# A two-block network in one kernel: the first four projections taken from x instead of from its norm, and other places in the queues for shift sums, a turn and activations of the mixer

## The chip, the cores and the metric

One core of a Trainium2 chip runs the whole program in one launch. The metric is the device time of one execution in microseconds, the median of several. A core has TensorE (matrix products), VectorE, ScalarE and GpSimd, each with its own queue of instructions that it works off in order, SyncE, which issues most DMAs, and 16 DMA engines. Engines wait for one another through semaphores, and a waiting instruction holds up everything queued behind it on its engine.

## What is computed

All in float32, 512 tokens by 1024 channels. The first layer is differential attention with 16 heads; then come an adaptively modulated ffn, a token mixer (pools, convolutions, gated delta rule in 8 heads) and a second ffn. Cut to what matters here:

```python
h = rms_norm(x, g)                          # x * rsqrt(mean(x*x)+eps) * g
q, k, v, z = split(h @ w_in)                # 4 x 2048 columns
q = rms_norm(q per 64, q_g) / 8; k = rms_norm(k per 64, k_g)
o = differential_attention(q, k, v, alibi)
x = x + (rms_norm(o, head_g) * 0.8 * silu(z)) @ w_out
shift, scale, gate = split(silu(c) @ ada_w + ada_b)        # for 3 sublayers
h = rms_norm(x, g0) * (1 + scale0) + shift0
x = x + 0.5 * gate0 * (silu(h @ w_gate) * (h @ w_up)) @ w_out1
h = rms_norm(x, g1) * (1 + scale1) + shift1
x = x + gate1 * token_mixer(h)              # h @ w -> pools, conv q/k/v, b/a, z, gates
h = rms_norm(x, g2) * (1 + scale2) + shift2
x = x + 0.5 * gate2 * ffn2(h)
out = rms_norm(x, final_g)
```

## The kernel before

Channels lie on the 128 partitions, tokens along the free axis, so x is eight chunks X[0..7] of 128x512. A **tile** is 128 output columns: for each step k (128 rows of the weight) TensorE makes three products (lines 1111, 1112, 1114): high part of the weight by high part of the operand, high by low, low by high, all rounded to a faster format. So every operand is split: ScalarE rounds (hi_of), VectorE takes the difference (lo_of). The weights of eight steps, 512 KB, are a **slot**. SyncE fetches slots in order into four buffers; the step `split` rounds one, three slots ahead of its use. A step of eight k is thus followed by its output (`out_...`) and a split.

The order is written by class Plan: a list of steps, and each engine walks the same list and takes from it what is its own. In the mixer and in attention, small steps are put between the k of the tiles by number: `at(tick, step)`, where a tick is one k, or SCHED. A step's place in the list is its place in the queue of **every** engine that has a part in it.

**Start** (lines 1024 to 1064, 1411, 1828 to 1866). SyncE fetches small data, constants, the eight chunks of x, then the slots. ScalarE squares the chunks, TensorE sums them into ps[7], ScalarE makes the root (logarithm and exponential), VectorE scales each chunk by gain and root, ScalarE rounds, VectorE subtracts: eight chunks in turn, with three splits behind the third. Then `two` runs q0 and k0 alternating, and v0 follows. `rstd` norms a head's q and k (a sum on TensorE, line 1162, from the parts that `sq_lo` finishes), `scores`, `weigh`, `turnw` and `pv` are the attention proper, `ada` computes the modulation from weights that GpSimd fetches.

**Later norms** (`raw_start`). The last residual chunk is late, so the first two or three tiles behind a norm run on x times gain ("raw", rhs "r"); their results are multiplied by the root, and the shift's part is added as a vector: `shift_row` (VectorE, line 1464, straight from the fetched weights) and `shift_sum` (TensorE sums the rows, line 1128; VectorE copies the result, line 1470). `norm_rs` makes the root, `norm_c` a run of chunks of h (VectorE 1479 and 1483, ScalarE 1899), needed from the first tile with rhs "h" on. Before, `shift_sum` stood in the last residual tile.

**Mixer.** Two raw pool tiles, a narrow tile ba (16 columns), pool 2, `baturn` (TensorE turns ba; ScalarE and VectorE make beta and g from it, a chain of small operations), pool 3, with `pool_mid` products in between (line 1224; GpSimd fetches their weights), `decays`. Then conv tiles for k, q and v: `out_conv` evicts, `conv_taps` (VectorE 1696 to 1701) follows 2 ticks behind the tile's last k, `conv_act` (ScalarE 2039, with `conv_sq` 2046) 7 ticks, `v_turn` 13. Sessions of four heads follow: `l2_sum` (TensorE 1252), `l2`, `prep_x`, `prep_k`, `prep_q`; a triangular solve on VectorE whose data go out and back through memory; inverse and recurrence.

Of the kernel before, what the change touches and what calls it, by code (L numbers as in the profile page):

```python
# [19 lines left out]
NRAW = 4  # L20
# [110 lines left out]
class Plan:  # L131
# [52 lines left out]
    def two(self, t0, t1, then=None, ahead=False):  # L184
        self.slot(t0, 0)
        self.slot(t1, 0)
        for k in range(8):
            self.add("mm", t=t0, k=k)
            self.add("mm", t=t1, k=k)
        for t in (t0, t1):  # L190
            t.done = t.slots[-1] + 1
            if ahead:
                self.add("split", j=t.slots[0] + NSPL)
        for t in (t0, t1):
            self.add("out_" + t.kind, t=t, done=t.done, **t.more)
            if not ahead:
                self.add("split", j=t.slots[0] + NSPL)
            if t is t0 and then is not None:
                then()

# [12 lines left out]
    def raw_start(self, n, t0, t1, t2=None):  # L213
# [4 lines left out]
        for k in range(8):  # L218
# [3 lines left out]
            self.add("mm", t=t0, k=k)  # L222
# [39 lines left out]
    def norm(self, n, kind):  # L262
        self.add("norm", n=n, kind=kind, stat=8 + 2 * n, rs=self.sig("rs"), nv=8 * n, nl=8 * n)
        if kind != "out":
            for name in ("nv", "nh", "nl"):
                self.count[name] = self.count.get(name, 0) + 8

    def attention(self):
# [3 lines left out]
        for c in range(8):  # L272
            self.square(0, c)
        self.norm(0, "plain")
        add("rnd", both=[sig("rnd"), sig("rnd")])
        st = [{} for _ in range(HEADS)]
        qk_free, rs_free = [("nl", 8)] * 4, [("nl", 8)] * 4
# [4 lines left out]
        def tile(kind, col, **d):  # L282
            return Tile(kind, src("l0_w_in", col), pb.take()[1], "h", None, n=0, **d)
# [13 lines left out]
        def v(h):  # L297
            d = dict(h=h, ve=sig("ve"))
            st[h]["v"] = d
            t = tile("v", 4096 + 128 * h, d=d)  # L300
# [76 lines left out]

        small = {}
        for i in range(HEADS + 3):
# [10 lines left out]
            if i < HEADS:  # L390
                put(SCHED["lo"][1], sq_lo, i, "k")
# [14 lines left out]
            for n in range(NADA):  # L406
                if (SCHED["ada"] + 21 * n) // 24 == i:
                    put((SCHED["ada"] + 21 * n) % 24, ada, n)
# [26 lines left out]
    def out0(self):  # L435
# [18 lines left out]
        def square(c):  # L454
# [7 lines left out]
              (7, 8): lambda: self.shift_row(1, 2, first + 2), (7, 13): lambda: self.shift_sum(1, 3)}  # L462
# [14 lines left out]
    def ffn(self, sub, w_in, w_out):  # L477
# [31 lines left out]
        for c in range(8):  # L509
            r = sig("xr")  # L510
            t = Tile("res", src(w_out, 128 * c, 22), pb.take()[1], "a", ("xr", r), c=c, xr=r, sub=sub, f=f, back=None)
            for k in self.steps_of(t):
# [6 lines left out]
                if n == 1 and c == 7 and k == 16:  # L519
                    self.shift_sum(2, 2)  # L520
# [4 lines left out]
    def mixer(self):  # L525
# [17 lines left out]

        self.raw_start(n, pool(0, "r"), pool(1, "r"))
        add("feed_pool")
        t = Tile("ba", src("mix_w_in_2", 4608, cols=16), wk.take()[1], "h", ("bd", 1), n=n)
        self.whole(t)
        for k in self.steps_of(pool(2)):
            if k == 5:
                pool_mid(0)  # L550
        add("baturn", bank=wk.take()[1])
        self.move("saved")
        for k in self.steps_of(pool(3)):
            if k == 5:
                pool_mid(1)
# [51 lines left out]
        def conv(which, h):  # L607
# [85 lines left out]
        at(7, pool_mid, 2)  # L693
        at(11, lambda: add("decays", bank=wk.take()[1]))
# [1577 lines left out]
```

## Time and profile before

| | |
|---|---|
| three runs | 1914.41, 1915.87, 1916.69 us; median 1915.87 |
| the profiled execution | 1915.09 us |
| its span, first to last instruction | 1913.3 us |
| TensorE products | 1873.1 us busy (98%), 8923 |
| VectorE | 988.9 us (52%) |
| ScalarE | 815.8 us (43%) |
| GpSimd | 124.2 us (6%) |
| mean granted TensorE clock | 0.994 |

A page of the profile gives the busy time of each engine, the span in 40 slices, the DMA queues, the chain that ended last and the costliest groups of instructions. Line numbers are the kernel's; L1820 and L1404 are the helpers of all roundings and differences. Since TensorE is busy nearly throughout, the views that matter are those of its idle time: a list of what each engine waited for, and timelines in order of time.

### The profile page before, as it was taken

How to read it: one execution, taken by the hardware profiler on the slowest of the kernel's cores; microseconds unless marked ns; L12 is line 12 of the kernel's file. 1: busy time of each engine (PE TensorE's matmuls, PEld its weight loads, DVE VectorE, ACT ScalarE, POOL GpSimd, SP SyncE). 2: the span in 40 equal slices, each digit the busy share in tenths (PEclk: the TensorE clock that was granted, in tenths of full speed). 3: DMA queues.
4: the chain of work that ended last, by engine and by line, in shares of the span. 5: the costliest groups of instructions: out<-in, count | busy, mean ns of one | idle time of the engine just before them, and what ended most of it. 6: DMA issues, size and time to landing. Idle time of an engine off the chain costs nothing.

```text
span 1913.3 us, 22366 instructions
## 1 busy us (share of the span) xinstructions
PE 1873.1 (98%) x8923; PEld 1452.5 (76%) x8923; DVE 988.9 (52%) x1764; ACT 815.8 (43%) x1325; POOL 124.2 (6%) x148
## 2 busy tenths in 40 slices
PE   7999999999999999999999999999999999999997
PEld 4666666666788788888886777677888878888886
DVE  4566667666544643333347566854434673333322
ACT  5466556656643342222324555434432342222221
POOL 0111111110001000000010011000000100000000
PEclk9999999999999999999999999999999999999999
DMA  5334334332233132222223222221023322322221
GB/s 213 147 144 150 137 143 155 143 144 99 78 118 123 69 110 99 94 96 92 99 95 117 93 72 88 84 94 34 34 96 113 121 89 99 99 93 97 97 93 62
DMA packets 56526, 201.95 MB, mean 106 GB/s; under 512 B 6478, under 2 KB 6934, under 8 KB 55784
## 3 DMA queue, kind: packets, MB, share of 16 engines
q1 hardware_dynamic: 44616, 158.32, 23.6%
q0 software_dynamic: 11808, 42.21, 6.1%
q8 instruction: 71, 1.16, 0.2%
q14 instruction: 31, 0.25, 0.0%
HBM read 195.23 MB, written 5.28 MB: 105 GB/s over the span
## 4 chain that ended last, share of the span: by engine, by line
PE 76%; DVE 12%; ACT 9%; issue 2%; DMA 1%; POOL 0%; DVEq 0%; SPq 0%; ACTq 0%
PE ps L1111 22%; PE ps L1114 22%; PE ps L1112 22%; ACT wH L1820 2%; DVE wL L1404 2%; PE ps L1209 2%; PE ps L1173 1%; DVE a L1533 1%; PE ps L1197 1%; DVE a L1699 1%; ACT a L1931 1%; PE ps L1185 1%; PE ps L1245 1%; PE ps L1144 1%; DVE b L1464 1%
## 5 line engine op out<-in xcount | busy, mean ns | idle before, releaser
L1111 PE MATMUL ps<-hH,wH 128*128 128x512 f32 x1592 | 649.3, 408 | 7.6 <-ACT wH L1820 5.9
L1114 PE MATMUL ps<-hH,wL 128*128 128x512 f32 x1592 | 623.7, 392 | 0.2 <-DVE wL L1404 0.2
L1112 PE MATMUL ps<-hL,wH 128*128 128x512 f32 x1592 | 622.6, 391 | 0.0
L1404 DVE TENSOR_TENSOR wL<-wr,wH 128x1024 fp32r<-128x1024 f32 (+2 forms) x285 | 345.1, 1212 | 526.7 <-ACT wH L1820 526.5
L1820 ACT ACTIVATE wH<-wr 128x1024 fp32r<-128x1024 f32 (+2 forms) x285 | 295.0, 1036 | 239.8 <-PE ps L1114 226.1
L1111 PEld LDWEIGHTS ps<-hH,wH 128*128 128x128 f32 x1592 | 299.7, 188 | 104.6 <-issue 36.2
L1114 PEld LDWEIGHTS ps<-hH,wL 128*128 128x128 f32 x1592 | 299.0, 188 | 66.2 <-DVE wL L1404 1.1
L1112 PEld LDWEIGHTS ps<-hL,wH 128*128 128x128 f32 x1592 | 300.0, 188 | 62.6 <-issue 6.2
L1111 PE MATMUL ps<-gffn,wH 128*128 128x512 f32 x400 | 157.4, 394 | 1.0 <-DVE xT L1618 1.0
L1112 PE MATMUL ps<-gffn,wH 128*128 128x512 f32 x400 | 156.3, 391 | 0.0
L1114 PE MATMUL ps<-gffn,wL 128*128 128x512 f32 x400 | 156.2, 390 | 0.0
L1931 ACT ACTIVATE a<-a,tiny 128x128 f32<-128x128 f32 (+3 forms) x128 | 71.0, 555 | 154.4 <-DVE tiny L1537 154.3
L1820 ACT ACTIVATE gffn<-affn 128x512 fp32r<-128x512 f32 x44 | 27.8, 632 | 187.1 <-DVE affn L1610 183.9
L1111 PEld LDWEIGHTS ps<-gffn,wH 128*128 128x128 f32 x400 | 75.3, 188 | 17.6 <-DVE xT L1618 1.4
L1112 PEld LDWEIGHTS ps<-gffn,wH 128*128 128x128 f32 x400 | 75.5, 189 | 16.0 <-issue 0.5
L1114 PEld LDWEIGHTS ps<-gffn,wL 128*128 128x128 f32 x400 | 75.5, 189 | 16.0
L1610 DVE TENSOR_TENSOR affn<-ps,affn 128x512 f32<-128x512 f32 x42 | 29.0, 691 | 104.6 <-PE ps L1114 102.9
L1111 PE MATMUL ps<-g,wH 128*128 128x512 f32 x192 | 74.9, 390 | 0.0
L1114 PE MATMUL ps<-g,wL 128*128 128x512 f32 x192 | 74.8, 389 | 0.0
L1112 PE MATMUL ps<-g,wH 128*128 128x512 f32 x192 | 74.7, 389 | 0.0
L1986 ACT ACTIVATE affn<-ps 128x512 f32<-128x512 f32 x40 | 23.9, 597 | 119.0 <-PE ps L1114 119.0
L2157 POOL TENSOR_TENSOR affn<-affn 128x512 f32<-128x512 f32 x12 | 18.5, 1545 | 691.8 <-ACT affn L1847 691.8
(301 smaller groups left out, 2049.6 us busy)
## 6 DMA issues: line engine op xcount, KB each, us to landing
wr<-wst SPq DMA_DIRECT2D x268, 512.0 KB, 3.5
a<-wfd POOLq DMA_DIRECT2D x54, 512.0 KB, 4.7
xT<-wfd POOLq DMA_DIRECT2D x18, 512.0 KB, 7.0
wr<-wst SPq DMA_DIRECT2D x16, 384.0 KB, 3.0
xT<-xin SPq DMA_DIRECT2D x8, 256.0 KB, 4.9
xT<-xin SPq DMA_DIRECT2D x2, 1024.0 KB, 6.1
xsave<-xT SPq DMA_DIRECT2D x1, 2048.0 KB, 7.9
c<-wfd POOLq DMA_DIRECT2D x8, 256.0 KB, 3.1
```

The lines of the kernel that those rows point to most:

```text
L1111: e.matmul(o, hi, xh[k], start=k == 0, stop=False)
L1112: e.matmul(o, hi, xl[k], start=False, stop=False)
L1114: i = e.matmul(o, lo, xh[k], start=False, stop=k == t.nk - 1)
L1144: e.matmul(ps[7][:], C("one1024"), square_view(d), start=d["n"] == 0 and d["c"] == 0, stop=d["c"] == 7).then_inc(s["stat"], 1)
L1173: i = e.matmul(ps[d["banks"][m]][:, a["at"]:a["at"] + n], qn[h % 2][64 * m:64 * m + 64, 128 * qb:128 * qb + 128], kn[h % 2][64 * m:64 * m ...
L1185: i = e.transpose(b4(b, qb - kb), Wr[h % 2][:, a:a + 128], C("ident"))
L1209: i = e.matmul(ps[7][32 * j:32 * j + 1, :], csil[:, k:k + 1], ada_buf[a % ADA_BUFS][:, 512 * (j % 2):512 * (j % 2) + 512], start=k == 0, s ...
L1404: e.tensor_tensor(dst, x, hi.bitcast(F32), ALU.subtract).then_inc(s[name], 1)
L1610: e.tensor_tensor(v, ps[t.bank][:], f["sg"][j % 2], ALU.mult).then_inc(s["fu"], 1)
L1820: e.activation(dst, x, ACT.Copy).then_inc(s[name], 1)
L1931: e.activation(v, v, ACT.Exp, bias=mx[:, m:m + 1], accum_out=rsum[:, m:m + 1]).then_inc(s["ex"], 1)
L1986: e.activation(v, ps[t.bank][:], ACT.Silu).then_inc(s["fg"], 1)
```

## The change

- **Start.** `first_tiles` replaces the squares, the norm and `two`. The chunks are multiplied by gain and split (raw 0), each followed by its square; q0, k0, v0 and q1 (the q tile of head 1, taken from the next round) run on them. Slots 0 and 1 are fetched between chunks of x. Norm chunks come in pairs between the outputs of the four tiles. The results are multiplied by the root on VectorE. The first `ada` moves ten steps back, and silu(c) is made from an exponential.
- **shift_sum** moves into `raw_start`, in front of its step k = 6, for all three norms. The first tile's last step goes ahead of the second's step 6. In the mixer norm_c is cut 4 and 4 instead of 5 and 3.
- **Mixer's head.** ba and pool 2 are interleaved; `baturn` stands behind the last k of ba for ScalarE and VectorE, and TensorE's turn becomes `ba_turn` at tick 3. The pool_mid steps, decays and the fetch of pool weights get other places.
- **Convs.** conv_act at 10 ticks, v_turn at 15. Before the second ffn the shift rows go a tile earlier.

```diff
@@ Plan
-        self.norm(4, "out")
+        self.out_norm()
@@ raw_start
             if k == 2:
                 self.last_square()
                 self.raw(n, 7)
-            self.add("mm", t=t0, k=k)
+            if k == 6:
+                self.shift_sum(n, len(tiles))
+            if k < 7:
+                self.add("mm", t=t0, k=k)
+            if k == 6:
+                self.add("mm", t=t0, k=7)
             self.add("mm", t=t1, k=k, raw=self.sig("rm") if k < 7 else None)
...
-        self.add("norm_c", n=n, c0=0, c1=5, rs=rs, raw=t1)
+        first = 4 if n == 2 else 5
+        self.add("norm_c", n=n, c0=0, c1=first, rs=rs, raw=t1)
         self.add("split", j=t0.slots[0] + NSPL)
-        self.add("norm_c", n=n, c0=5, c1=8, rs=rs, raw=t1)
+        self.add("norm_c", n=n, c0=first, c1=8, rs=rs, raw=t1)
         self.add("split", j=t1.slots[0] + NSPL)
@@ new
+    def first_tiles(self, tq, tk, tv, tq1):
+        free = [("rs", 0)] * 4
+        def chunk(c):
+            self.raw(0, c)
+            free[c % 4] = self.square(0, c, v=("first", c % 4), free=free[c % 4])
...
+        chunk(0)
+        chunk(1)
+        self.add("split", j=0)
+        mm(tq, 0, 1)
+        chunk(2)
+        chunk(3)
+        self.add("split", j=1)
+        mm(tq, 2, 3)
+        for c in range(4, 8):
+            chunk(c)
+        self.add("split", j=2)
+        mm(tq, 4, 5, 6, 7)
+        mm(tk, *range(8))
+        mm(tv, *range(8))
+        rs = self.sig("rs")
+        self.add("norm_rs", n=0, stat=8, rs=rs)
...
+        mm(tq1, *range(8))
...
+        self.chunks(0, 0, 2, rs)
+        self.add("split", j=3)
+        self.add("out_qk", t=tq, done=tq.done, rs=rs, **tq.more)
+        self.chunks(0, 2, 4, rs)
+        yield "q"
+        out(tk)
+        self.chunks(0, 4, 6, rs)
+        yield "k"
+        self.chunks(0, 6, 8, rs)
+        out(tv)
+        yield "q1"
+        out(tq1)
@@ attention
-                    self.two(qk(0, 0), qk(0, 1), lambda: sq_lo(0, "q"))
-                    for step in range(16):
+                    first = [qk(0, 0), qk(0, 1), v(0), qk(1, 0)]
+                    for t in first:
+                        t.rhs = "r"
+                    start = self.first_tiles(*first)
+                    sq_lo(0, next(start))
+                    sq_lo(0, next(start))
+                    next(start)
+                    tiles = []
+                elif i == 1:
+                    while step < 8:
                         run(step)
-                    step = 16
-                    tiles = tiles[2:]
+                        step += 1
+                    first[3].more["d"]["sum_free"] = sq_free[1]
+                    for _ in start:
+                        pass
+                    tiles = tiles[1:]
@@ out0
-              (7, 8): lambda: self.shift_row(1, 2, first + 2), (7, 13): lambda: self.shift_sum(1, 3)}
+              (7, 8): lambda: self.shift_row(1, 2, first + 2)}
@@ mixer
+        add("feed_pool", done=self.count["wb"] + 1)
         self.raw_start(n, pool(0, "r"), pool(1, "r"))
-        add("feed_pool")
-        t = Tile("ba", src("mix_w_in_2", 4608, cols=16), wk.take()[1], "h", ("bd", 1), n=n)
-        self.whole(t)
-        for k in self.steps_of(pool(2)):
-            if k == 5:
-                pool_mid(0)
-        add("baturn", bank=wk.take()[1])
+        ba = Tile("ba", src("mix_w_in_2", 4608, cols=16), wk.take()[1], "h", ("bd", 1), n=n)
+        second = pool(2)
...
+        for t, k in [(ba, k) for k in range(4)] + [(second, k) for k in range(4)] + [(t, k) for k in range(4, 8) for t in (ba, second)]:
+            self.mm(t, k)
+            if t is ba and k == 7:
+                turn = wk.take()[1]
+                add("baturn", bank=turn)
         self.move("saved")
         for k in self.steps_of(pool(3)):
             if k == 5:
-                pool_mid(1)
+                pool_mid(0)
...
-                    at(clock[0] + 7, conv_act, a)
+                    at(clock[0] + 10, conv_act, a)
                     if which == "v":
-                        at(clock[0] + 13, v_turn, h)
+                        at(clock[0] + 15, v_turn, h)
...
-        at(7, pool_mid, 2)
-        at(11, lambda: add("decays", bank=wk.take()[1]))
-        at(15, pool_mid, 3)
+        at(3, pool_mid, 1)
+        at(3, lambda: add("ba_turn", bank=turn))
+        at(13, pool_mid, 2)
+        at(14, lambda: add("decays", bank=wk.take()[1]))
+        at(20, pool_mid, 3)
...
-            if 3 <= c < 6:
-                self.shift_row(3, c - 3, first + c - 3)
-            elif c == 6:
-                self.shift_sum(3, 3)
+            if 2 <= c < 5:
+                self.shift_row(3, c - 2, first + c - 2)
@@ sync
             for c in range(8):
                 e.dma_start(c5(xT, c), x_d[:, 512 * c:512 * c + 512]).then_inc(s_x[c], 16)
+                if c in (0, 2):
+                    weights(c // 2)
@@ vector
+                elif what == "out_qk":
+                    t, d2 = d["t"], d["d"]
+                    if t.rhs == "r":
+                        w.wait_ge(s["slot"], t.done)
+                        w.wait_ge(s["rs"], d["rs"])
+                        e.tensor_tensor(qk_raw[d2["m"] % 4], ps[t.bank][:], norm_views(0)[0], ALU.mult).then_inc(s["qe"], 1)
@@ tensor
-                elif what == "baturn":
+                elif what == "ba_turn":
@@ gpsimd
                 elif what == "feed_pool":
-                    w.wait_ge(s["nl"], 24)
+                    w.wait_ge(s["al"], 22)
+                    w.wait_ge(s["wb"], d["done"])
```

## Rows read from the trace of the kernel before

**Rows 1.** The page: busy time of TensorE; the rounding helper: busy, mean ns.
```profile
PE 1873.1 (98%) x8923; PEld 1452.5 (76%) x8923; DVE 988.9 (52%) x1764; ACT 815.8 (43%) x1325; POOL 124.2 (6%) x148
...
L1820 ACT ACTIVATE wH<-wr 128x1024 fp32r<-128x1024 f32 (+2 forms) x285 | 295.0, 1036 | 239.8 <-PE ps L1114 226.1
```

**Rows 2.** What TensorE waited for: who, line, for whom: total us, times, longest.
```profile
PE ps L1252 <- ACT a L2046: 3.4, 3, 1.8
...
PE ps L1111 <- DVE hL L1483: 1.7, 2, 1.1
PE ps L1128 <- DVE b L1464: 1.7, 1, 1.7
...
PE ps L1224 <- DMA c<-wfd: 1.5, 1, 1.5
PE ps L1258 <- ACT o L2039: 1.4, 1, 1.4
PE ps L1111 <- DVE xT L1618: 1.0, 1, 1.0
```

**Rows 3.** Timeline, TensorE, 0 to 75: start, duration, instruction, [idle before it].
```profile
21.45 0.79 PE L1111 MATMUL ps<-hH,wH 128*128 128x512 f32 x1 [5.88 <-ACT wH L1820]
...
68.84 0.47 PE L1162 MATMUL ps<-g1a,rnd 128*128 128x512 f32 x1 [1.28 <-DVE g1a L1404]
```

**Rows 4.** Window 652 to 656: busy us (count) of each engine, clock, DMA.
```profile
652.00:656.00 4.00, 4.00 (x12) 3.10 (x11) 2.58 (x3) 2.19 (x3) 0.00 (x0) 0.58 0.14 23
```

**Rows 5.** Timelines of the start, all engines, and ScalarE at 51.
```profile
1.65 3.89 SPq L1027 DMA_DIRECT2D xT<-xin  x8
...
7.26 1.24 ACT L1847 ACTIVATE a<-xT 128x512 f32<-128x512 f32 x2 [0.17 <-DMA xT<-xin]
...
15.60 0.69 ACT L1856 ACTIVATE a<-ps,cst 128x512 f32<-128x512 f32 x1 [2.75 <-PE ps L1144]
...
16.98 1.41 DVE L1436 SCALAR_TENSOR_TENSOR a<-xT,sml,a 128x512 f32<-128x512 f32 x2 [11.97 <-ACT a L1858]
...
31.22 1.80 POOL L2131 DMA_DIRECT2D a<-wfd  x3 [14.61 <-DVE hL L1404]
...
51.61 0.63 ACT L1909 ACTIVATE a<-a 128x512 f32<-128x512 f32 x1
```

**Rows 6.** Timelines of the first raw start, VectorE and TensorE, and TensorE at 1024.
```profile
659.67 1.41 DVE L1479 SCALAR_TENSOR_TENSOR affn<-xT,tiny,affn 128x512 f32<-128x512 f32 x2 [4.35 <-ACT affn L1888]
...
667.40 1.22 DVE L1404 TENSOR_TENSOR wL<-wr,wH 128x1024 fp32r<-128x1024 f32 x1 [0.20 <-ACT wH L1820]
...
663.55 0.39 PE L1111 MATMUL ps<-gffn,wH 128*128 128x512 f32 x1
...
671.72 0.39 PE L1111 MATMUL ps<-hH,wH 128*128 128x512 f32 x1
...
1024.87 0.39 PE L1111 MATMUL ps<-hH,wH 128*128 128x512 f32 x1
```

**Rows 7.** Timelines of the mixer's head, VectorE, then TensorE at conv tile 3.
```profile
1020.96 1.41 DVE L1479 SCALAR_TENSOR_TENSOR a<-xT,tiny,a 128x512 f32<-128x512 f32 x2 [3.01 <-ACT a L1888]
...
1044.24 1.20 DVE L1404 TENSOR_TENSOR wL<-wr,wH 128x1024 fp32r<-128x1024 f32 x1
...
1050.36 0.18 DVE L1645 TENSOR_TENSOR tiny<-ps,sml 128x32 f32<-128x32 f32 x1
...
1055.08 0.15 DVE L1631 COPY a<-a 128x1 f32<-128x1 f32 x1
...
1070.34 0.39 PE L1111 MATMUL ps<-hH,wH 128*128 128x512 f32 x1
```

**Rows 8.** Timelines of the mixer, ScalarE, and VectorE at the solve.
```profile
1052.23 0.21 ACT L2014 ACTIVATE tiny<-tiny 128x32 f32<-128x32 f32 x1
1052.46 1.28 ACT L2016 ACT_TABLE_LOAD   x1
...
1074.11 0.63 ACT L2039 ACTIVATE o<-o 128x512 f32<-128x512 f32 x1 [4.05 <-DVE o L1701]
...
1184.41 0.09 DVE L1736 MEMSET a<- 128x32 f32 x1 [6.25 <-DMA a<-dsol]
```

More of the change, by code:

```diff
@@ L182, in whole @@
                 then()
[L184 to L187, printed above, removed]
-            self.add("mm", t=t0, k=k)
[L189 to L199, printed above, removed]
     def raw(self, n, c):
@@ L260, in square, with out_norm, chunks, mm @@
         return free
[L262 to L266, printed above, removed]
+    def out_norm(self):
+        self.add("norm", n=4, stat=16, rs=self.sig("rs"))
+    def chunks(self, n, c0, c1, rs, raw=None):
+        self.add("norm_c", n=n, c0=c0, c1=c1, rs=rs, raw=raw)
+    def first_tiles(self, tq, tk, tv, tq1):
[3 more added lines that the diff above has]
+            free[c % 4] = self.square(0, c, v=("first", c % 4), free=free[c % 4])
+        def mm(t, *ks):
+            for k in ks:
+                self.add("mm", t=t, k=k)
+        tiles = [tq, tk, tv, tq1]
+        for t in tiles:
+            self.slot(t, 0)
+            t.done = t.slots[-1] + 1
+        chunk(0)
[14 more added lines that the diff above has]
+        self.add("norm_rs", n=0, stat=8, rs=rs)
+        self.add("rnd", both=[self.sig("rnd"), self.sig("rnd")])
+        for name in ("nv", "nh", "nl"):
+            self.count[name] = 8
+        mm(tq1, *range(8))
+        def out(t):
+            self.add("out_" + t.kind, t=t, done=t.done, rs=rs, **t.more)
+            self.add("split", j=t.slots[0] + NSPL)
+        self.chunks(0, 0, 2, rs)
[10 more added lines that the diff above has]
+        out(tq1)
     def attention(self):
@@ L271, in attention @@
         add("start")
[L272 to L275, printed above, removed]
         st = [{} for _ in range(HEADS)]
-        qk_free, rs_free = [("nl", 8)] * 4, [("nl", 8)] * 4
+        qk_free, rs_free = [("rs", 1)] * 4, [("nl", 8)] * 4
         sq_free = [0, 0]
@@ L280, in attention, with tile @@
         n_qk = [0]
-        def tile(kind, col, **d):
-            return Tile(kind, src("l0_w_in", col), pb.take()[1], "h", None, n=0, **d)
+        def tile(kind, col, bank=None, **d):
+            return Tile(kind, src("l0_w_in", col), pb.take()[1] if bank is None else bank, "h", None, n=0, **d)
         def qk(h, w):
@@ L299, in v @@
             st[h]["v"] = d
-            t = tile("v", 4096 + 128 * h, d=d)
+            t = tile("v", 4096 + 128 * h, 4 if h == 0 else None, d=d)
             t.freed = ("ve", d["ve"])
@@ L376, in z_early, with ada_step @@
             return t
+        def ada_step(n):
+            return SCHED["ada"] + (21 * n if n else 10)
         small = {}
@@ L390, in attention @@
             if i < HEADS:
-                put(SCHED["lo"][1], sq_lo, i, "k")
+                if i:
+                    put(SCHED["lo"][1], sq_lo, i, "k")
             if o3 >= 0:
@@ L960, in norm_views @@
             if n == 0:
-                return qn[0], [c5(t, j) for t in Wr for j in range(2)]
+                return row, [c5(t, j) for t in Wr for j in range(2)]
             if n == 2:
@@ L1884, in _ @@
                     n, rs = d["n"], norm_views(d["n"])[0]
+                    w.wait_ge(s["first"], 16)
                     w.wait_ge(s["stat"], d["stat"])
@@ L1898, in _ @@
                         w.wait_ge(s["nv"], 8 * n + c + 1)
-                        e.activation(c5(hH, c), tmp[c % 2], ACT.Identity, bias=shift_col(n, c)).then_inc(s["nh"], 1)
+                        if n == 0:
+                            hi_of(c5(hH, c), tmp[c % 2], "nh")
+                        else:
+                            e.activation(c5(hH, c), tmp[c % 2], ACT.Identity, bias=shift_col(n, c)).then_inc(s["nh"], 1)
                 elif what == "out_qk":
@@ L1902, in _ @@
                     m = d["m"]
-                    w.wait_ge(s["slot"], t.done)
-                    w.wait_ge(s[d["free"][0]], d["free"][1])
-                    e.activation(qk_raw[m % 4], ps[t.bank][:], ACT.Copy).then_inc(s["qe"], 1)
+                    if t.rhs == "h":
+                        w.wait_ge(s["slot"], t.done)
+                        w.wait_ge(s[d["free"][0]], d["free"][1])
+                        e.activation(qk_raw[m % 4], ps[t.bank][:], ACT.Copy).then_inc(s["qe"], 1)
                     w.wait_ge(s["qe"], d["qe"])
```

145 lines of the change are left out of this document (62 added, 83 removed).

## The prediction

> **What bounds the kernel now.** Read the page first: TensorE is busy for 1873.1 us of 1913.3 [rows 1]. The kernel goes by TensorE's program, so an edit is worth what it does to TensorE's 40.2 us of idle time and to the time at half clock. The list of what TensorE waited for comes next: after the start the large entries are 3.4 (sums of the mixer's k and q heads), 1.7 (the mixer's h), 1.7 (a shift sum), 1.5 (pool weights), 1.4 (v turn) and 1.0 (a residual) [rows 2]. The timeline places the two at the beginning: 5.88 us before the first product at 21.45, 1.28 at 68.84 [rows 3]. Last, the clock: behind the 1.69 us wait for the shift sum, the window 652 to 656 shows a granted 0.58, between 1.2 and 2.4 GHz [rows 4]. At 0.58 four microseconds do the work of 2.3, so 1.7 us go there on top of the wait. A step k of a tile (three products) takes 0.68 us: twelve of them lie between 663.55 and 671.72 [rows 6].
>
> **Part 1, the start.** Before: the eight squares, the root, the whole norm's first chunk and a split all precede the first product. After: four tiles (q0, k0, v0, q1) run on x times gain, and only their results are multiplied by the root. The products begin at about 11 us and are no longer late. What is late next is the other end of the same work: ScalarE and VectorE now do the eight chunks of the norm, five splits and four evictions in turn, and head 0's scores wait for the last of it.
>
> When are the squares done (S)? Eight x DMAs were issued in 3.89 us, 0.49 each; chunk 2 was waited for until 7.26 [rows 5]. Weights 0 and 1 (512 KB each, two chunks' worth) now go ahead of x1 and x3, so x1 lands near 8 and x7 near 13.4 (estimate from these rows). ScalarE then has 16 passes of about 0.64 and three splits of 1.04 [rows 1, 5]; its last square ends near 18.9, TensorE's last sum near 20.4 behind two pairs of steps. S = 20.4 (before: 15.6).
>
> From S, in queue order, with 0.65 for a pass, 1.0 for a split on ScalarE, 1.2 for its half on VectorE and 2.75 for a pair of chunks (two scalings 1.41, then 0.65 and 0.69) [rows 1, 5, 7]: root 1.4; pair 2.75; split, q0's eviction, square and rounding 3.5 (7.65); chunks 2 and 3 beside it 1.95 (9.6); sq_lo and k0 with split 4.7 (14.3); pair 2.7; sq_lo 0.6; pair 2.7 (20.3); two logarithms and two exponentials of head 0 behind the next split 3.0 (23.3); two products and q1's eviction 1.5 (24.8). So q1's square starts at 20.4+24.8 = 45.2. Its counterpart before started at 51.61 [rows 5], and the chain from there to the wait at 68.84 [rows 3] has the same steps. Gain 6.4. TensorE is there by 42 for head 0's scores and idles some 3.5 us inside this; a dip of its clock behind that idle may take 0.5: **5.9**. Bounds 4 (S two later) and 8 (squares as soon as x lands).
>
> Other queues: SP issues all moved DMAs with no new wait; the rest of the constants go one weight later, still ahead of their first reader. In part 3 GpSimd's pool feed moves ahead of raw_start and waits for the copy of the shift sum; nothing is queued behind it, and its data are there some ten microseconds earlier than now. The ada feed on GpSimd still waits for the eighth chunk (31.22 before [rows 5], about 41 now); its first user moves back ten steps to about 52, and nothing but tables stands behind it. The two activation table loads that fall away lie before x0 lands: nothing; if x0 were there earlier they would be worth their 1.28 each.
>
> **Part 2, first shift sum.** It leaves the last tile of out0 for step 6 of raw_start. The wait of 1.7 [rows 2] and the dip's 1.7 [rows 4] go. But VectorE's copy of that sum now stands in its queue ahead of norm_c and waits for TensorE to reach step 6. Before, norm_c began at 659.67; TensorE comes to step 6 at 663.55 and needs 0.6 for the sum, so it begins at 664.35, 4.7 later [rows 6]. The split for the first h tile ended at 668.62 and ends at 673.3; the tile starts at 671.7+0.6 and needs it 0.45 later: 0.5 of stall, and 0.9 more over the next splits and chunks 7 and 8. Gain 3.4-1.4 = **2.0** (1 to 3.4).
>
> **Part 3, the head of the mixer.** The same barrier: norm_c began at 1020.96; step 6 is at 1024.87, so 1025.4 now [rows 6, 7]. From the start of norm_c to the end of the split of conv tile 0 VectorE had 24.48 us of unbroken work (1020.96 to 1045.44) [rows 7], so that split ends at 1049.9. TensorE, without the waits for h and the pool weights and with ba and pool 2 interleaved, is through pool 3 by 1047.5: a stall of about 2. Then **baturn**: on ScalarE and VectorE it now stands ahead of pool 2's output and of the split for conv tile 1, and waits for TensorE's ba_turn, which comes only behind three steps of conv tile 0 and a pool product, at 1052.7. VectorE's part of baturn took 4.72 (1050.36 to 1055.08), the pool output and split ahead of it 4.91 (from 1045.45) [rows 7]. So the split of conv tile 1 ends at 1053.0+4.7+4.9 = 1062.6, and TensorE, ready at 1056.6, idles 6.0. Conv tile 2 finds its split (about 1068.0) in time. Adding up: tile 1's rest 6.3 with pool 2 and decays, tile 2 with pool 3 6.3: conv tile 3 starts at 1075.2 against 1070.34 [rows 7], less 0.36 for the shift sum that used to stand earlier: 4.5 lost, with 3.2 of old waits already given back. A clock dip behind an idle of 6 costs 1.7 [rows 4] to 3: **6.8 lost**. Bounds: 9 lost; 3.5 gained if VectorE isn't late.
>
> The loads of activation tables inside baturn are taken as 1.28 each: the one at 1052.46 follows an activation of 0.21 at 1052.23 with nothing between [rows 8].
>
> **Part 4, the convs.** conv_act moves from 7 to 10 ticks behind its tile. Before, ScalarE waited 4.05 us at 1074.11 for the taps and held back the next tile's eviction and split, on which the next taps wait [rows 8]: a lock step of 6.8 us per tile against TensorE's 5.4. Now the next split goes first. The waits for k and q sums (3.4) and for the v turn (1.4) [rows 2] were its price. The stretch behind the wait of 6.25 for the solve's data [rows 8] stays full on VectorE, so I take **3.0** of 4.8 (0 to 4.8).
>
> **Part 5, second norm of the ffn.** Shift rows one tile earlier free VectorE, and the 1.0 [rows 2] goes; the barrier costs 1.4 as in part 2: **0.4 lost**. The final norm is the same code.
>
> **Sum.** -5.9 -2.0 +6.8 +0.4 -3.0 = -3.7. The profiled execution took 1915.09 (span 1913.3, 1.8 around it), 0.8 under the median of the runs and within them. 1915.1-3.7 = **1911.4**.
>
> **The rivals.**
> A, the forecast, chance 0.44; its own range is 1907.5 to 1915.
> B, VectorE is not late in the mixer's head. For it: the split of conv tile 1 had some 7.7 us in hand: it ended at 1050.4, and two tiles with a pool product and decays (12.2) back from 1070.34 the tile began at 1058.1 [rows 7]. Against: 4.5 of barrier plus 4.7 of baturn are more, and TensorE comes earlier. Then part 3 gains 3.5: 1915.1-5.9-2.0-3.5+0.4-3.0 = 1901.1. Chance 0.27.
> C, VectorE alone, not the lock step, made the conv waits; part 4 is nothing: 1914.4. Chance 0.10.
> D, the change doesn't do what it says: the four tiles start early, but the serial norm chain eats them (S at 22 and each pair near 3.5, as with an exposed hand-over). Part 1 gives 2: 1915.3. Chance 0.09.
> E, slower: the mixer head's lag is still open when the transfers of the solve are sent. VectorE already waited 6.25 for them [rows 8]; lag is passed on at its full size and a dip comes with it, 2.7+1.7, and part 4 gives nothing, part 1 its low 4: 1914.4+1.9+4.4 = 1920.7. It decides once the taps of the eighth k tile are over 2 us later against TensorE than before. Chance 0.08.
>
> F, the switches of activation table inside baturn cost a second 1.28 each, once nothing else fills the time around them: 2.6 more before the split of conv tile 1, 1914.0. Chance 0.02, since rows 8 show none of it: the load began as the activation before it ended. The Trainium skill (ScalarE: Activation LUTs, What ACT_TABLE_LOAD costs) counts a load of 1283 ns and a drain of 1380 ns for each switch; the trace agrees with the load and shows no drain, and by the page the sum would be 1914.2.
>
> **How the numbers follow.** A measurement of this kernel tells some 0.2% from no change: under 1912.0 is faster, over 1919.7 slower. Faster: B and 0.23 of A, 0.5. Slower: E and no more, 0.08. The rest, 0.42, lies between. The range takes in A, C, D, F and most of B: 1901 to 1917.
>
> **What would show it.** Right: first product near 11; an idle of 3 to 4 us before head 0's first scores; the rstd wait of 68.84 near 62.4; no wait at the shift sum; norm_c in the mixer starting right behind the copy of the shift sum; an idle of about 6 us before the third product of conv tile 1, ended by VectorE's split; no waits for conv squares. Wrong: conv tile 1 without idle (then B), or the rstd wait over 65 (then D).

## The result, and the profile after

Seven runs of the changed kernel gave 1908.22 to 1911.04 us, median 1910.1; seven of the kernel before beside them 1914.14 to 1916.69, median 1914.71. The ratio is 0.9973, 95% interval 0.9963 to 0.9982: faster by 0.27%, and the whole interval is below 1. The forecast was 1911.4 in 1901 to 1917, which is 3.7 under the profiled execution of before; the medians differ by 4.6 and the profiled executions by 5.2. The profiled execution took 1909.85 us, with a span of 1908.0 against 1913.3. The first part of the page after, busy time and instructions of each engine:

```profile
span 1908.0 us, 22387 instructions
...
PE 1873.6 (98%) x8923; PEld 1451.8 (76%) x8923; DVE 995.9 (52%) x1778; ACT 818.0 (43%) x1328; POOL 124.2 (7%) x148
```

TensorE's busy time is that of before [rows 1]; what fell is its idle time. The list of what TensorE waited for, after (line, releaser: total, times, longest):

```profile
PE ps L1180 <- DVE wL L1472: 5.9, 4, 3.5
PE ps L1199 <- DMA cst<-const: 3.4, 1, 3.4
PE ps L1205 <- ACT a L1908: 3.4, 2, 2.9
PE ps L1241 <- DVE a L1584: 2.4, 1, 2.4
PE ps L1177 <- ACT wH L1882: 1.8, 1, 1.8
...
PE ps L1377 <- DVE a L1810: 1.5, 1, 1.5
...
PE ps L1177 <- DVE hL L1543: 1.0, 2, 0.6
PE ps L1177 <- DVE xT L1650: 0.9, 1, 0.9
```

The waits for conv squares, shift sum, v turn and pool weights [rows 2] are gone. New are 5.9 and 1.8 for splits of weights and 2.4 for the first scores.

To see where the time went, take instructions that exist in both kernels, at the borders of the stages, and subtract their starts. TensorE's timeline, before:

```profile
605.74 0.23 PE L1217 MATMUL ps<-cst,b 72*128 72x72 f32 x1
...
1017.66 1.02 PE L1141 MATMUL ps<-affn,cst 128*128 128x512 f32 x2
...
1085.35 1.02 PE L1252 MATMUL ps<-a,cst 128*128 128x512 f32 x2
...
1322.95 0.66 PE L1341 MATMUL ps<-cst,a 128*128 128x128 f32 x4 [0.25 <-ACT o L2059]
...
1901.04 1.02 PE L1141 MATMUL ps<-affn,cst 128*128 128x512 f32 x2
```

and after (the turn of the modulation in out0, the sum of squares ahead of the mixer, the first sum of a conv head, the first recurrence step, the last sum of squares):

```profile
600.21 0.23 PE L1285 MATMUL ps<-cst,b 72*128 72x72 f32 x1
...
1010.80 1.02 PE L1211 MATMUL ps<-affn,cst 128*128 128x512 f32 x2
...
1085.15 1.02 PE L1320 MATMUL ps<-a,cst 128*128 128x512 f32 x2
...
1316.98 0.66 PE L1409 MATMUL ps<-cst,a 128*128 128x128 f32 x4 [0.25 <-ACT o L2109]
...
1895.82 1.02 PE L1211 MATMUL ps<-affn,cst 128*128 128x512 f32 x2
```

| stretch ending at | lead over before, us | this stretch | forecast |
|---|---|---|---|
| modulation turned (start and attention) | 5.53 | -5.5 | -5.9 |
| sum of squares ahead of the mixer | 6.86 | -1.3 | -2.0 |
| first sum of a conv head | 0.20 | +6.7 | +6.8 |
| first recurrence step | 5.97 | -5.8 | -3.0 |
| last sum of squares | 5.22 | +0.8 | +0.4 |
| sum | | -5.2 | -3.7 |

The 0.36 of the mixer's shift sum lie ahead of the second border before and behind it after. The prediction's part 3 takes them out, so its -2.0 and +6.8 stand beside -1.0 and +6.3.

The mixer's head, where 6.7 were lost, on three engines, after. VectorE at the shift sum, ScalarE at baturn:

```profile
1018.54 0.16 DVE L1527 COPY tiny<-ps 128x4 f32<-128x4 f32 x1 [7.45 <-PE ps L1194]
1018.62 1.41 DVE L1536 SCALAR_TENSOR_TENSOR a<-xT,tiny,a 128x512 f32<-128x512 f32 x2
```

```profile
1039.50 1.28 ACT L2059 ACT_TABLE_LOAD   x1
1046.29 0.20 ACT L2059 ACTIVATE tiny<-ps 128x32 f32<-128x32 f32 x1 [5.50 <-PE ps L1298]
1046.74 0.23 ACT L2061 ACTIVATE tiny<-tiny 128x32 f32<-128x32 f32 x1 [0.26 <-DVE tiny L1707]
1046.99 1.28 ACT L2062 ACT_TABLE_LOAD   x1
...
1050.54 1.05 ACT L1882 ACTIVATE wH<-wr 128x1024 fp32r<-128x1024 f32 x1
```

and TensorE in the conv tiles:

```profile
1043.15 0.50 PE L1180 MATMUL ps<-hH,wL 128*128 128x512 f32 x1 [1.61 <-DVE wL L1472]
...
1045.83 0.42 PE L1298 MATMUL ps<-cst,a 16*128 16x16 f32 x4
...
1051.73 0.47 PE L1177 MATMUL ps<-hH,wH 128*128 128x512 f32 x1 [1.79 <-ACT wH L1882]
...
1055.97 0.80 PE L1180 MATMUL ps<-hH,wL 128*128 128x512 f32 x1 [3.54 <-DVE wL L1472]
```

norm_c starts 0.08 behind the copy of the shift sum, for which VectorE stood idle 7.45 (it waited for TensorE to reach step 6; this wait in VectorE's queue is called the barrier below). ScalarE stands 5.50 at baturn until TensorE's turn at 1045.83; only then does the rounding for conv tile 1 run, at 1050.54, and TensorE idles 1.79 + 3.54 = 5.3 us for it.

### The profile page after: what moved, and what is told of

The parts are those of the page before. It is cut to its first block, busy times and chain, and to the rows that moved or that the text cites. A ratio compares the mean times of both kernels' runs of the same rounds, so it can differ in the third digit from the quotient of the medians.

```text
span 1908.0 us, 22387 instructions
## 1 busy us (share of the span) xinstructions
PE 1873.6 (98%) x8923; PEld 1451.8 (76%) x8923; DVE 995.9 (52%) x1778; ACT 818.0 (43%) x1328; POOL 124.2 (7%) x148
## 4 chain that ended last, share of the span: by engine, by line
PE 83%; DVE 9%; ACT 6%; issue 2%; DMA 0%; SPq 0%; DVEq 0%; ACTq 0%
PE ps L1177 24%; PE ps L1180 23%; PE ps L1178 23%; ACT wH L1882 2%; PE ps L1277 2%; DVE wL L1472 1%; PE ps L1313 1%; DVE a L1595 1%; PE ps L1241 1%; ACT a L1981 1%; PE ps L1265 1%; PE ps L1253 1%; PE ps L1320 1%; PE ps L1230 1%; DVE g1a L1472 1%
## 5 line engine op out<-in xcount | busy, mean ns | idle before, releaser
L1177 PE MATMUL ps<-hH,wH 128*128 128x512 f32 (+1 forms) x1560 | 637.1, 408 | 2.8 <-ACT wH L1882 1.8
L1180 PE MATMUL ps<-hH,wL 128*128 128x512 f32 (+1 forms) x1560 | 611.8, 392 | 6.1 <-DVE wL L1472 5.9
L1178 PE MATMUL ps<-hL,wH 128*128 128x512 f32 (+1 forms) x1560 | 610.3, 391 | 0.0
L1177 PEld LDWEIGHTS ps<-hH,wH 128*128 128x128 f32 (+1 forms) x1560 | 293.5, 188 | 99.0 <-issue 38.3
L1180 PEld LDWEIGHTS ps<-hH,wL 128*128 128x128 f32 (+1 forms) x1560 | 293.1, 188 | 73.4 <-DVE wL L1472 10.0
L1178 PEld LDWEIGHTS ps<-hL,wH 128*128 128x128 f32 (+1 forms) x1560 | 293.8, 188 | 60.7 <-issue 6.2
L1177 PE MATMUL ps<-g,wH 128*128 128x512 f32 x224 | 89.4, 399 | 0.0
L1180 PE MATMUL ps<-g,wL 128*128 128x512 f32 x224 | 87.7, 392 | 0.0
L1178 PE MATMUL ps<-g,wH 128*128 128x512 f32 x224 | 87.7, 391 | 0.0
L1178 PEld LDWEIGHTS ps<-gffn,wH 128*128 128x128 f32 x400 | 75.1, 188 | 15.8 <-issue 0.5
L1180 PEld LDWEIGHTS ps<-gffn,wL 128*128 128x128 f32 x400 | 75.1, 188 | 15.8
```

Source lines behind the costliest of these rows:

```text
L1177: e.matmul(o, hi, xh[k], start=k == 0, stop=False)
L1178: e.matmul(o, hi, xl[k], start=False, stop=False)
L1180: i = e.matmul(o, lo, xh[k], start=False, stop=k == t.nk - 1)
```

## Experiments

Each time is a median of 4 to 11 runs; each ratio is to runs of the kernel before on the same chip. "Loss of the head" is the time from the sum of squares ahead of the mixer to the first sum of a conv head in the profiled execution, less the 67.7 of before (1017.66 to 1085.35); the changed kernel's is 6.7.

Differences below 2 us between two runs' end times need care. The kernel before was run again beside each set, and its five medians lie between 1914.08 and 1915.55. The start of the changed kernel, with no edit in it, ended at 598.95 (x2) to 601.01 (x5), measured at the turn of the modulation. And behind TensorE's wait of 1.50 at the mixer's inverse, which all thirteen traces have, the first recurrence step comes 19.9 us later in five of them (before, after, x1, x2, x11), with a clock dip, and 18.4 in the other eight, with none. No edit is made there. So where the trace of x3 to x10 is compared with that of the changed kernel, 1.5 us is this dip and not the edit.

**x1: the new start alone.** Shift sums, mixer and convs are as before.

> The kernel before with the new start alone (first four tiles on x, moved ada steps, table loads, order of the first DMAs); shift sums, head of the mixer and convs as before. My theory: the start is worth what the changed kernel showed at the rstd sum (68.84 to 62.92, 5.9), and nothing behind it eats it: 5.4 to 5.9 under the kernel before, some 1909.3, with the waits of 1.7 (shift sum), 3.4 (k and q sums) and 1.4 (v turn) all still there. Rival D' (the queues behind are late anyway and swallow the start's gain in the attention or at out0): within 2 of before, 1913 or more.

1911.97 us, ratio 0.9983 (0.9974 to 0.9991). Less than expected. The lead was 5.89 at the shift sum (644.00 against 649.89) and 3.71 at the next sum of squares. Between them stands the old wait of 1.69, and a longer stretch at half clock behind it. Windows of TensorE in x1 (busy, count, granted clock, DMA share, GB/s):

```profile
640.00:644.00 4.00, 2.31 (x11) 1.00 0.41 131
644.00:648.00 4.00, 3.23 (x12) 0.63 0.00 0
648.00:652.00 4.00, 3.98 (x10) 0.51 0.35 109
652.00:656.00 4.00, 4.00 (x15) 1.00 0.07 27
```

0.37x4 + 0.49x4 = 3.4 us of work are lost there, against 1.7 before [rows 4]. Three of the eleven runs took 1908.1 to 1908.6 and eight 1911.2 to 1912.9. A dip that is sometimes short and mostly long would give that, but only one of the eleven has a trace.

**x9: x1 with the shift sum two steps later**, which tests that reading.

```diff
-(7, 13): lambda: self.shift_sum(1, 3)
+(7, 15): lambda: self.shift_sum(1, 3)
```

> x1 (the start alone) with the first shift sum two steps later in out0's last tile, at step 15 and not 13. In x1 the start's 5.9 were there up to the shift sum (644.00 against 649.89) and 3.7 behind it: the same wait of 1.69, but the clock at 0.63 and 0.51 in the two windows of 4 us behind it, 3.4 us of work lost against 1.7 in the kernel before. My theory: the missing 2.2 is this longer dip, called by the wait; with 1.36 of the wait covered the dip goes as a whole: 1.4 + 3.4 under x1 at the sum of squares, near 1907.3. Rival (the 2.2 were lost in the order of out0 for another reason): only the 1.4 of the wait, near 1910.6.

1906.34 us, ratio 0.9951 (0.9939 to 0.9964): 0.32% below x1. The wait was 0.33, the clock 1.00 in all windows from 640 to 652, and the lead at the sum of squares 8.29. All five runs lie below all eleven of x1. So the wait and the dip behind it took back part of the start's gain in x1. The wait doesn't always bring the dip, though: x6, which is the kernel before up to the convs, has the same 1.69 at the same place and the clock at 1.00 in all windows from 640 to 664. Whether the new start makes the dip longer, or its length just differs between executions, isn't shown; x6 speaks for the second.

**x2: VectorE's copy of the shift sum behind the first part of norm_c.**

```diff
+        self.add("norm_c", n=n, c0=0, c1=first, rs=rs, raw=t1)
+        self.add("shift_copy", **self.shift)
...
-                elif what == "shift_sum":
+                elif what == "shift_copy":
                     w.wait_ge(s["modt"], d["modt"])
```

> The changed kernel, with VectorE's copy of each shift sum moved behind the first part of norm_c, so that norm_c no longer waits for TensorE's step 6; TensorE's part stays at step 6, and the pool feed waits for TensorE's sum and not for the copy. My theory: norm_c of the mixer starts 4.5 us earlier (near 1014.1 instead of 1018.62), the waits of 0.39, 0.58 on h and 1.61 at conv tile 0 go, 0.37 at each ffn norm goes; the idle of 5.3 inside conv tile 1 stays, since baturn still waits for ba_turn: 2.5 to 3.5 under the changed kernel, near 1907. Rival (the barrier is the whole loss of the mixer's head): the idle of conv tile 1 goes too, 7 to 9 under, near 1902. Rival (VectorE has slack there and the barrier costs nothing): 0 to 0.5 under, 1910.

1902.45 us, ratio 0.9939 (0.9927 to 0.9951): 7.6 below the changed kernel, the size of the first rival's 7 to 9, but not by its mechanism: the 1.80 and 3.53 inside conv tile 1 stayed. By the borders: the loss of the head fell by 3.1 (my 2.5 to 3.5), each ffn behind a norm was 1.57 shorter (363.07 to 361.50 and 360.33 to 358.76), and 1.3 came from a start that ran better in this execution without an edit (598.95 against 600.21 at the turn of the modulation). By the borders the edit itself is worth 6.3. I had expected 0.37 for each ffn, from the only wait listed there. The next two lines, TensorE after, show why that was wrong:

```profile
664.78 0.50 PE L1180 MATMUL ps<-hH,wL 128*128 128x512 f32 x1 [0.37 <-DVE wL L1472]
...
670.37 0.40 PE L1178 MATMUL ps<-hL,wH 128*128 128x512 f32 x1
670.74 0.51 PE L1180 MATMUL ps<-hH,wL 128*128 128x512 f32 x1
```

The third product of the next tile is late too, 0.37 behind the second where 0.23 is the rule, but it starts inside the modelled end of the product before it, so no wait is listed. Compared start by start, x2 gains 0.6, 0.5 and 0.4 around the third products of three tiles in turn (664.78, 670.74, 676.56).

**x3: baturn's ScalarE and VectorE part at tick 3.**

```diff
             if t is ba and k == 7:
                 turn = wk.take()[1]
-                add("baturn", bank=turn)
...
         at(3, lambda: add("ba_turn", bank=turn))
+        at(3, lambda: add("baturn", bank=turn))
```

> The changed kernel, with the ScalarE and VectorE part of baturn moved behind the outputs of pools 2 and 3 and the splits for conv tiles 1 and 2, to the step at which TensorE does ba_turn; the barrier of the shift sum stays. My theory: baturn's wait for ba_turn held back the split of conv tile 1; now the idle of 5.3 there goes and its clock dip (1.7), the 1.6 at conv tile 0 stays, and some 1 to 2 come back as baturn's 4.7 of VectorE push the conv outputs: 4 to 6 under the changed kernel, near 1905. Rival (VectorE is short of time in the whole head, and the place of baturn does not matter): the idle moves to conv tile 2 or 3 or to the first k sums at its size, 0 to 1.5 under, near 1909.

1906.4 us, ratio 0.9952 (0.9938 to 0.9965): 3.7 below the changed kernel, a little less than the 4 to 6 that I expected. The 5.3 inside conv tile 1 went. But baturn now ended later, at 1057.4 on VectorE, and TensorE's decays, at tick 14, waited for it:

```profile
1057.42 0.41 PE L1304 MATMUL ps<-tiny,cst 128*128 128x32 f32 x2 [3.03 <-DVE tiny L1731]
```

So over half of the stall came back as a new wait at another reader. The head lost 4.3, which is 2.3 less than in the changed kernel; 1.5 of the 3.7 is the dip at the inverse that this execution doesn't have. A wait of 0.78 for the solve's data, at 1264.87, is new here and takes back part.

**x4: x2 and x3 together.**

> x2 and x3 together. My theory: the two losses of the mixer's head are separate and add: no idle of over 0.5 in the first four conv tiles, 8 to 9 under the changed kernel, near 1901.5, which is the 1901.1 of rival B in the prediction. Rival (one loss seen twice, VectorE's lag): no more than the larger of the two alone, near 1905.

1899.92 us, ratio 0.9925 (0.9913 to 0.9937). The head lost 1.7, so the gains of 3.1 and 2.3 nearly add (5.0). I expected no idle over 0.5 in the head; the wait for decays was 2.98.

**x8: x4 with decays at tick 24.**

```diff
-        at(14, lambda: add("decays", bank=wk.take()[1]))
+        at(24, lambda: add("decays", bank=wk.take()[1]))
```

> x4 (copy behind norm_c, baturn late) with TensorE's decays moved from tick 14 to tick 24. In x4 the only wait of the head was that of decays for VectorE's last step of baturn, 2.98 at 1052.03, with the clock at 0.89, 0.50 and 0.76 in the three windows of 4 us behind 1048, 3.4 us of work lost. My theory: both go, and nothing else waits for decays before the first prep_x at tick 51: 4 to 6 under x4, near 1895. Rival (VectorE is full there and the stall moves to the first conv outputs or k sums): 0 to 2 under x4.

1894.3 us, ratio 0.9894 (0.9878 to 0.9909). As expected: no wait of TensorE is left from 645 to 1284, its clock is 1.00 in all windows of the head, and the head **gains** 4.4 (1008.92 to 1072.18, 63.3) where the changed kernel loses 6.7. Of the 16.0 by which its profiled execution is shorter than the changed kernel's, 11.1 are the head, 3.1 the two ffn norms, 1.5 the dip at the inverse that isn't there and 0.3 the start. This is the fastest version, 20.6 us under the kernel before and 15.8 under the changed one, with the same computation.

**x7: the order of before in the head, barrier kept.**

```diff
-        add("feed_pool", done=self.count["wb"] + 1)
         self.raw_start(n, pool(0, "r"), pool(1, "r"))
...
+        add("feed_pool", done=self.count["wb"])
+        t = Tile("ba", src("mix_w_in_2", 4608, cols=16), wk.take()[1], "h", ("bd", 1), n=n)
+        self.whole(t)
+        for k in self.steps_of(pool(2)):
+            if k == 5:
+                pool_mid(0)
+        turn = wk.take()[1]
+        add("baturn", bank=turn)
+        add("ba_turn", bank=turn)
...
-        at(3, lambda: add("ba_turn", bank=turn))
...
+        at(11, lambda: add("decays", bank=wk.take()[1]))
```

> The changed kernel with the order of before in the head of the mixer (ba, then pool 2 with pool 0's product, baturn with its turn behind pool 2, pool 3, decays at tick 11); the shift sums stay at step 6, so norm_c still waits for them, and the pool feed stays early. My theory: the split of conv tile 1 had 7.7 us in hand and the barrier takes 4.5 of it, so the idle of 5.3 goes and the waits of VectorE's lag (1 on h, and 1 to 2 at pool 0's product, which stands one tile earlier) are what is left: the head loses 2 to 3 and not 6.7, near 1906. Rival (the barrier alone makes the head late, whatever its order): the head still loses 5 to 7, near 1910.

1907.31 us, ratio 0.9959 (0.9947 to 0.9972); the head lost 5.5, which is the rival's 5 to 7 and not my 2 to 3. No stall inside conv tile 1, as I said, but two that I had not seen:

```profile
1028.67 0.59 PE L1174 MATMUL ps<-hH,wH 128*16 128x512 f32 x1 [2.82 <-DVE hL L1540]
...
1042.13 0.44 PE L1295 MATMUL ps<-cst,a 16*128 16x16 f32 x4 [2.28 <-DVE a L1701]
```

The narrow tile ba reads all eight chunks of h, and with norm_c 4.5 later the later ones are not there when ba stands alone. The new interleaving of ba and pool 2 covers most of that: the changed kernel waits 0.39 and 0.58 there and has no wait of 2.82. The stall inside conv tile 1 came with baturn's new place and not with the interleaving.

**x5: the changed kernel with conv_act at 7 and v_turn at 13. x6: the kernel before with them at 10 and 15.** One is the mirror of the other.

```diff
-                    at(clock[0] + 10, conv_act, a)
+                    at(clock[0] + 7, conv_act, a)
                     if which == "v":
-                        at(clock[0] + 15, v_turn, h)
+                        at(clock[0] + 13, v_turn, h)
```

> The changed kernel with conv_act again 7 ticks and v_turn 13 ticks behind their tile. My theory (lock step of ScalarE and VectorE, part 4): the waits of 3.4 for the k and q sums and 1.4 for the v turn come back, at least 4.7 over the changed kernel, near 1915. Rival C (VectorE alone made those waits): they do not come back, within 1 of 1910.

> The kernel before with conv_act 10 and v_turn 15 ticks behind their tile and nothing else. My theory: the four waits (0.37, 1.23, 1.78, 1.35) go and nothing takes their place, since the rest of the mixer has the same order: 4.7 to 5.6 under the kernel before, near 1909. Rival C: within 1 of before. Rival: the gain needs the lag of the new head and is not there from before's: 2 or less.

x5 took 1914.47 us, ratio 0.9999 (0.9990 to 1.0008), 4.4 over the changed kernel; x6 took 1909.06, ratio 0.9968 (0.9956 to 0.9981), 5.9 under the kernel before. Rival C falls in both, and so does x6's rival that the gain needs the new head's lag. The waits are back in x5, 3.7 in all where before had 4.7 (TensorE):

```profile
1133.14 1.10 PE L1320 MATMUL ps<-a,cst 128*128 128x512 f32 x2 [0.56 <-ACT a L2096]
...
1176.11 1.10 PE L1320 MATMUL ps<-a,cst 128*128 128x512 f32 x2 [1.23 <-ACT a L2096]
...
1214.65 1.10 PE L1320 MATMUL ps<-a,cst 128*128 128x512 f32 x2 [0.51 <-ACT a L2096]
...
1228.01 0.63 PE L1326 MATMUL ps<-cst,o 128*128 128x128 f32 x4 [1.37 <-ACT o L2089]
```

and in x6 there is none between the first sum of a conv head and the inverse. That stretch took 217.7 us before (1085.35 to 1303.04), 211.9 after (1085.15 to 1297.03), 216.7 in x5 and 211.9 in x6. So the two tick numbers are worth 5.8 of TensorE's time with the old head and 4.8 with the new one, and all the rest of the change together is worth nothing that can be told (x5 against before). The end time of x6 is no clean measure of them: its trace also lost 1.6 in the head, where the wait for pool weights was 2.81 and not 1.47, and had no dip at the inverse, 1.5.

**x10: x8 with v0's output and its split behind head 0's exponentials. x11: x10 with the last four steps of q1's tile behind head 0's sums.** These ask what the new wait of 2.38 at the first scores is made of.

```diff
         self.chunks(0, 6, 8, rs)
+        yield "v"
         out(tv)
         yield "q1"
```

(and the third `next(start)` of the plan now comes with the first q1 steps; x11 puts `mm(tq1, *range(4, 8))` right behind the new yield).

> x8 with head 0's v output and its split moved behind head 0's logarithms and exponentials, so that ScalarE's 1.04 for that split no longer stands between the norm's last chunk and the roots of head 0, on which the first scores wait (2.38 at 44.25 in x8). My theory of the start: this wait is the serial chain of ScalarE and VectorE, so it gets 1.0 shorter, and the dip behind it (clock 0.59 in the window 44 to 48, 1.6 us) is smaller or gone: 1.0 to 2.7 under x8, near 1892.3. Rival (the wait is TensorE's own sums, done late, and not this chain): 0 to 0.3 under x8.

> x10 with the last four steps of q1's tile moved behind head 0's sums, which so come 2.7 us earlier on TensorE. x10 showed that ScalarE's split was not what the first scores wait for: the wait stayed 2.38 and the logarithm started at 41.53, idle, behind TensorE's sums at 40.01, while in x8 it started at 40.99 behind a full ScalarE queue with the sums at 39.44. My theory now: two chains of equal length end there, TensorE's sums behind q1's tile and ScalarE's queue with the v split, and only both together shorten the wait: the logarithm comes 0.5 to 0.9 us earlier (the norm's last roundings on ScalarE end at 40.6), the wait at the first scores falls to 1.5 to 1.9, TensorE gains 0.5 to 0.9 at the sums of head 1, and up to 1.7 more where the dip goes too: 1892 to 1894. Rival (latency of the steps from the sums to the scores alone): the wait stays 2.38 and the time 1894.5.

x10: 1894.64 us, ratio 0.9891 (0.9876 to 0.9907), the wait again 2.38: my theory of ScalarE's split was wrong. x11: 1896.7 us (1892.8 to 1898.3), ratio 0.9903 (0.9886 to 0.9919), no faster (its trace has the dip at the inverse, x10's hasn't). Its sums came at 36.53 and 38.10 against 40.01, but its logarithm was 0.8 earlier only because the norm ran 0.8 earlier in this execution. VectorE and ScalarE in x11 show what it waited for:

```profile
39.31 1.35 DVE L1478 TENSOR_TENSOR hL<-a,hH 128x512 fp32r<-128x512 f32 x2
```

```profile
40.76 1.27 ACT L1976 ACTIVATE xT<-ps,cst 128x512 f32<-128x512 f32 x2 [0.82 <-DVE hL L1478]
```

The logarithm starts 0.10 behind VectorE's last difference of the norm (39.31 + 1.35 = 40.66), and 0.10 and 0.14 behind it in x10 and x8. The code says why: the results of `rstd` go where x stood, and `rs_free` makes them wait for the norm's last chunk. So the eight chunks in turn on ScalarE and VectorE set the logarithm and with it the first scores, and neither the split nor TensorE's sums. This is read from the code and these gaps; no run moved the chunks themselves. x11's wait at the scores fell to 1.13 only because TensorE had more to do meanwhile; 0.96 and 1.82 appeared around it, and its stretch at half clock behind the scores went. TensorE is 0.8 ahead of x10 at the next sums (263.53 against 264.29), which is no more than the 0.8 by which this norm was earlier, so nothing is left for the edit. Whether another place for the logarithm would shorten the start wasn't tried.

## Why the prediction was right

The sign, the size and the forecast itself held (1911.4 for 1910.1), and case A was the one that came. But two steps missed in opposite directions, part 2 by 1 us and part 4 by 3, and in parts 1 and 3 misses inside the part cancelled. To that extent the closeness is luck.

**Part 1, start: right.** The first product on a chunk came at 10.51 (forecast 11). Squares were done at 20.4 in the forecast, and the root started at 20.98; q1's square at 45.2 in the forecast, and in the trace (ScalarE, after)

```profile
45.19 0.63 ACT L1959 ACTIVATE a<-a 128x512 f32<-128x512 f32 x1 [1.56 <-DVE a L1504]
```

The sum that waited at 68.84 [rows 3] stands at 62.92, without a wait, where 62.4 was forecast. The idle ahead of the first scores was 2.38, not 3.5, but the dip behind it cost 1.7 (clock 0.65 and 0.92 from 44 to 52), not 0.5: the two misses cancel. Gain 5.5 for 5.9; x1 shows 5.9 up to the first shift sum. With the same start, x5 and x2 have leads of 4.7 and 6.8 at the same border, and the start of before came 1.0 later in x6, so the 0.4 between forecast and trace says nothing. Rival D fell.

**Part 2, first shift sum: 1.0 for 2.0, the first step that missed.** The wait of 1.7 and the dip of 1.7 went, and the barrier cost 1.57 in x2 where the sum had 1.4. What the sum left out is that the next step comes 1.7 earlier too: TensorE now waits 0.85 for the last residual at 644.88 (the 0.9 in the list above), which was ready in time before. 3.4 less 1.57 and 0.85 is the measured 1.0. The question "what is late next" was asked of VectorE's queue and not of TensorE's next operand.

**Part 3, head of the mixer: right in place, in size partly by luck.** 6.3 lost for 6.8. norm_c right behind the copy, 1.61 at the third product of conv tile 0 (forecast 2), 5.3 inside conv tile 1 (6.0), ba_turn at 1045.83, which is 1052.7 less the lead of 6.9. But the sum held more misses, which nearly cancel. It put the waits on h as gone, and 0.97 of them stayed. It took the dip behind the stall at 2.3, and it cost 1.7. And it left out that the head of before had a dip of its own, behind the waits of 1.12 and 0.58, which goes; in two windows 0.22x4 + 0.21x4 = 1.7 us of work were lost there. Windows of TensorE before (busy, count, granted clock, DMA share, GB/s):

```profile
1032.00:1036.00 4.00, 3.07 (x10) 0.78 0.15 66
1036.00:1040.00 4.00, 4.00 (x15) 0.79 1.08 393
```

The other way, about 1.5 us of the loss stand in no list of waits, likely by the effect seen in x2: late starts that aren't listed as waits. The 24.48 us of VectorE in that stretch weren't quite unbroken, as the prediction has it: some 2.7 of them are short waits for ScalarE, which came again after, so the estimate held.

x2 and x3 share the loss out: 3.1 to the barrier, and 2.3 to baturn's place, net of the new wait of decays; with decays moved too it is 8.0 (x8 against x2). x7 shows that the old order would have lost 5.5 behind the same barrier. Rival B, no lateness, is not the changed kernel; x8 is: its head gains 4.4 (4.8 without the 0.36) where B said 3.5.

**Part 4, convs: mechanism right, term mis-sized.** 5.8 gained, where the sum had 3.0 and as its upper bound 4.8. This is the largest miss. I had cut the listed waits (0.37 + 1.23 + 1.78 + 1.35 = 4.7) by a third because VectorE looked full further on; nothing there became late. And the bound itself was too low, since a wait costs more than is listed: after's lead over before grows by 1.43 across the place of the wait of 1.23 and by 1.96 across that of 1.78, 0.2 more each. The likely reason is that idle time is counted only from the modelled end of the last product (0.39 long, where the next starts after 0.23). Four waits at 0.2 more make 5.5 of the 5.8. Rival C fell by x5 and x6.

**Part 5, second ffn norm: 0.8 lost for 0.4.** The 0.98 became 0.16 as forecast; the barrier cost 1.57 for 1.4.

**Rival E** did not come: the lag of the head (TensorE level with before at 1085) was not passed on, no wait for the solve's data appeared on TensorE. It isn't far off: x3 has one of 0.78. **Rival F** fell: three loads of 1.28 each at 1039.50, 1046.99 and 1048.63, and each activation starts as the load ends (1046.99 + 1.28, next at 1048.28). The first began 6.8 us ahead of the activation that needed it (1046.29), while that one waited for TensorE. The Trainium skill (ScalarE: Activation LUTs, What ACT_TABLE_LOAD costs) counts a drain of 1380 ns with every switch; ScalarE's own timeline here shows the load's 1.28 and no drain.

## What to carry over

Where all engines walk one list of steps, a step moved for one engine moves in the queues of all: a copy of 0.16 us, moved with its sum, held back VectorE's norm by 4.5 us in the mixer, and giving copy, baturn and decays places of their own (x8) was worth more than the change as a whole. When a stall goes, look for the next wait at the next reader (x3: conv tile 1, then decays) and at the same engine's next operand (part 2), and measure stretches between instructions that both kernels have, since here the list of waits counted each too low and left short ones out. A change of many parts is worth undoing part by part: two tick numbers alone gave as much as all of it.

## What the runs showed of the hardware

- The same wait of 1.69 us at the same place cost its own length and behind it three different things: 1.7 us of work in the kernel before (granted clock 0.58 in one window of 4 us), 3.4 in x1 (0.63 and 0.51 in two), and nothing in x6 (1.00 in all windows).
- TensorE's granted clock fell behind every wait of 2.2 us or more that was looked at: 2.38 in the start (after, 0.65 in the window 44 to 48), 2.82 in x7 (0.59), 2.98 in x4 (0.50). It didn't fall behind 1.13 and 1.82 in x11's start, nor behind 1.23, 1.35 and 1.78 in the convs of the kernel before. The waits of 1.12 and 0.58 close together at 1032 were followed by a dip in the kernel before and by none in x6, where the head's dip came only behind the next wait, 2.81 (0.83 and 0.74 from 1040 to 1048). The 1.50 at the inverse was followed by a dip in five of thirteen traces. So for waits of 1.1 to 1.8 us their length alone didn't tell whether a dip follows, and the same wait in the same code fell out both ways.
- Executions of the same start differ by up to 1.9 us on TensorE at the same sum (262.10 in x2, 263.21 after, 264.02 in x5), with no edit between them. Effects of that size need the borders of stages, not the end time.
